# An encoder block on one core: the values' low halves on VectorE, the last four value blocks tile by tile, and a bank for the keys' products

## What is computed

```python
A = jnp.where(strict, jnp.einsum('nbhid,nbhjd->nbhij', k_beta, k) * dec, 0.0)
attn = jnp.einsum('nbhid,nbhjd->nbhij', q, k) * dec
```

```python
act = jax.nn.gelu(jnp.einsum('ld,lkd->lk', xb, u_tab[e]), approximate=False)
y = jnp.einsum('lk,lkd->ld', act * g, v_tab[e])      # summed over heads
h = layer_norm(DEEPNORM_ALPHA * h + y, ln2_g, ln2_b)
return h[:, N_META:]
```

## Time and profile before

| | us |
|---|---|
| median of 3 runs (lowest to highest) | 2587.49 (2587.34 to 2589.34) |
| the profiled execution, and its span | 2584.99, 2583.2 |
| TensorE busy (matmuls) | 2412.5, 93% |
| VectorE, GpSimd, ScalarE busy | 1821.2, 1245.4, 1002.5 |
| value stage | from 2031 to 2583 of the span |
| delta stage, heads in the loop | 78 a head |

### The profile page before, as it was taken

How to read it: one execution, slowest core, us unless ns; L and a number is a source line. 1 busy time by engine, 2 the same in 40 slices (tenths; PEclk the granted TensorE clock), 3 DMA queues, 4 the chain that set the end, 5 groups by cost and what they waited for, 6 DMA issues and landing times. The chain is left out here.

```text
span 2583.2 us, 44561 instructions
## 1 busy us (share of the span) xinstructions
PE 2412.5 (93%) x14900; PEld 1436.5 (56%) x14993; DVE 1821.2 (71%) x3471; ACT 1002.5 (39%) x1759; POOL 1245.4 (48%) x740
## 2 busy tenths in 40 slices
PE   7999999979999999988999999989898899999997
PEld 5444444458888878874465555555565444444442
DVE  7534422047777777752432898889999699999999
ACT  3332332223333333323313333338888333333332
POOL 4321331321222121214513676666677588888885
PEclk9999999999999999999999999999999999999998
DMA  5321322221110001004321587778999799999996
GB/s 205 98 66 32 98 65 71 66 72 34 33 32 32 8 24 32 8 1 131 114 99 54 192 287 255 240 231 296 383 362 369 260 331 335 333 334 333 335 331 235
DMA packets 174309, 440.32 MB, mean 170 GB/s; under 512 B 17408, under 2 KB 83584, under 8 KB 174096
## 3 DMA queue, kind: packets, MB, share of 16 engines
q1 hardware_dynamic: 132752, 288.20, 32.5%
q0 software_dynamic: 36864, 134.23, 15.6%
q10 hardware_dynamic: 4608, 16.78, 1.6%
HBM read 395.11 MB, written 44.04 MB: 170 GB/s over the span
## 5 line engine op out<-in xcount | busy, mean ns | idle before, releaser
L2040 POOL TENSOR_TENSOR hid_u_lo<-hid_u,hid_u_hi 128x1024 bf16<-128x1024 f32 x128 | 295.4, 2308 | 195.6 <-ACT hid_u_hi L2024 183.0
L150 PE MATMUL bank<-hT_hi,hid_u_hi 128*128 128x384 bf16 x1024 | 335.3, 327 | 17.2 <-POOL hid_u_lo L2040 5.8
L214 POOL TENSOR_TENSOR w_shared_lo<-w_raw,w_shared_hi 128x1024 bf16<-128x1024 f32 x72 | 157.9, 2210 | 393.5 <-ACT w_shared_hi L209 393.5
L150 PE MATMUL bank<-hT_hi,hid_u_lo 128*128 128x384 bf16 x1024 | 335.0, 327 | 0.0
L150 PE MATMUL bank<-hT_lo,hid_u_hi 128*128 128x384 bf16 x1024 | 335.0, 327 | 0.0
L2786 DVE TENSOR_TENSOR ex_gated<-ex_gated,ex_grid 128x128 f32<-128x128 f32 x128 | 277.3, 2166 | 0.0
L150 PE MATMUL bank<-hT_hi,w_shared_hi 128*128 128x264 bf16 (+2 forms) x699 | 200.8, 295 | 7.6 <-ACT dn_conv_in L1419 4.5
L150 PE MATMUL bank<-hT_lo,w_shared_hi 128*128 128x264 bf16 (+2 forms) x699 | 200.7, 295 | 1.4 <-ACT ex_grid L2216 1.2
L150 PE MATMUL bank<-hT_hi,w_shared_lo 128*128 128x264 bf16 (+2 forms) x699 | 200.7, 295 | 0.3
L2739 ACT ACTIVATE ex_gated_hi<-ex_gated 128x384 bf16<-128x384 f32 x128 | 66.9, 522 | 340.8 <-DVE ex_gated L2786 340.8
L2754 POOL TENSOR_TENSOR w_shared_lo<-ex_v,w_shared_hi 128x1024 bf16<-128x1024 f32 x64 | 152.5, 2383 | 47.3 <-ACT w_shared_hi L2736 47.3
(11 more groups left out here) (507 smaller groups left out, 6084.1 us busy)
## 6 DMA issues: line engine op xcount, KB each, us to landing
hid_u<-in_peer_u SPq DMA_DIRECT2D x128, 512.0 KB
ex_v<-in_peer_v SPq DMA_DIRECT2D x128, 512.0 KB, 5.5
w_raw<-in_w_ret SPq DMA_DIRECT2D x60, 512.0 KB, 4.3
expert_hidden<-hid_gelu SPq DMA_DIRECT2D x128, 192.0 KB
ex_gated<-expert_hidden SPq DMA_DIRECT2D x128, 192.0 KB
w_raw<-in_w_dn SPq DMA_DIRECT2D x32, 512.0 KB, 3.5
expert_weights<-ex_grid ACTq DMA_DIRECT2D x32, 512.0 KB
ex_weights<-expert_weights SPq DMA_DIRECT2D x64, 256.0 KB
```

What stands on the lines that cost most here:

```text
L150: last = nc.tensor.matmul(out, left[l], right[r], start=start and i == 0, stop=stop and i == len(PASSES) - 1)
L214: self.nc.gpsimd.tensor_tensor(self.pairs[slot][1][:, m % 4, :, :], self.raw[:, m % self.RING, :, :], self.pairs[slot][0][:, m % 4, :, :], ...
L2040: self.nc.gpsimd.tensor_tensor(self.us[1][:, m % 2, :, :], self.u32[:, m % RING, :, :], self.us[0][:, m % 2, :, :], ALU.subtract).then_inc ...
```

## The change

In the value stage:

- VectorE makes the values' low half, in each step between the row addition and the gated low half. GpSimd's stream keeps the 128 gathers alone.
- A row is added two steps behind (`BEHIND`), so that two are left after the last step.
- TensorE takes the first 124 blocks as before. The last four (`LAST`) it takes unit by unit: all four blocks for tile 0's first half, then for its second, and so on, and it signals `summed` after each unit.
- A tile's normalisation follows its own moments.

In the delta stage `kk` moves from bank 1 to bank 5, `qk` comes after the meta tokens' product, and ScalarE copies `tk` ahead of `tv`.

```diff
         early = Banks(core, [("q", 2), ("pm0", 3), ("k", 3), ("pm1", 5), ("v", 5), ("pm2", 2), ("bf", 2),
-                             ("bb", 3), ("bm", 5), ("nq", 2), ("nk", 3), ("nm", 5), ("ss", 6), ("z", 6)], DH)
-        order = [("tv", 1), ("tk", 4), ("tm", 7), ("kk", 1), ("qk", 4), ("kkm", 7)]
+                             ("bb", 3), ("bm", 5), ("nq", 2), ("nk", 3), ("nm", 5), ("ss", 6), ("z", 6), ("kk", 5)], DH)
+        order = [("tv", 1), ("tk", 4), ("tm", 7), ("qk", 4), ("kkm", 7)]
...
-                        for name, dst in (("tv", v_tok), ("tk", k_tok)):
+                        for name, dst in (("tk", k_tok), ("tv", v_tok)):
...
+    BEHIND = 2
+    LAST = 4
...
+                def products(u, slot, ends):
+
+                    half, t = UNITS[u]
+                    for i, (l, r) in enumerate(PASSES):
+                        last = nc.tensor.matmul(core.banks[u][:, :], gs[l][:, slot, t * P:(t + 1) * P],
+                                                vs[r][slot][:, half * 512:(half + 1) * 512],
+                                                start=False, stop=ends and i == 2)
+                    return last
+
                 def step(n, m):
-                    last_one = isinstance(n, int) and n == BLOCKS - 1
-                    slot = m % SLOTS
+                    if isinstance(n, int) and n >= BLOCKS - LAST:
+                        return
                     for name in ("gated_hi", "gated_lo", "v_hi", "v_lo"):
                         pe.wait_ge(s[name], n + 1)
...
+                for u in range(len(UNITS)):
+                    for n in range(BLOCKS - LAST, BLOCKS):
+                        if u == 0:
+                            for name in ("gated_hi", "gated_lo", "v_hi", "v_lo"):
+                                pe.wait_ge(s[name], n + 1)
+                        last = products(u, n % SLOTS, n == BLOCKS - 1)
+                    last.then_inc(s["summed"], 1)
...
-                def low_half(n):
-                    pool.wait_ge(s["v_hi"], n + 1)
-                    nc.gpsimd.tensor_tensor(vs[1][n % SLOTS], v32[:, n % RING, :], vs[0][n % SLOTS],
-                                            ALU.subtract).then_inc(s["v_lo"], 1)
-
-                low_half(0)
...
-                    if n:
-                        low_half(n)
...
-                    if m:
-                        add_row(n - 1, m - 1 if m > 1 else 0)
+                    if m >= BEHIND:
+                        add_row(n - BEHIND, m - BEHIND)
+                    dve.wait_ge(s["v_hi"], n + 1)
+                    nc.vector.tensor_tensor(vs[1][m % SLOTS], v32[:, m % RING, :], vs[0][m % SLOTS],
+                                            ALU.subtract).then_inc(s["v_lo"], 1)
...
-                add_row(BLOCKS - 1, BLOCKS - 1)
+                for n in range(BLOCKS - BEHIND, BLOCKS):
+                    add_row(n, n)
...
                 for turn, tile in enumerate(ORDER):
                     moments(turn, tile)
-                    if turn == 1:
+                    if turn == 0:
                         dve.wait_ge(s["gb_in"], 32 + SPENT)
-                    if turn:
-                        normalise(turn - 1, ORDER[turn - 1])
-                normalise(NT - 1, ORDER[NT - 1])
+                    normalise(turn, tile)
```

More of the change, by code:

```diff
@@ L1225, in unit @@
                     early.wait_read(pe, "nq", h)
-                    for name, i in (("kk", 1), ("qk", 0)):
-                        bk.wait_free(pe, name, h)
-                        for t in range(NT):
-                            last = nc.tensor.matmul(out(name)[:, t * P:(t + 1) * P], qk[:, 1, tok_cols(t)],
-                                                    qk[:, i, tok_cols(t)], start=True, stop=True)
-                        bk.fills(name, last)
+                    early.wait_free(pe, "kk", h)
+                    for t in range(NT):
+                        last = nc.tensor.matmul(out("kk")[:, t * P:(t + 1) * P], qk[:, 1, tok_cols(t)],
+                                                qk[:, 1, tok_cols(t)], start=True, stop=True)
+                    early.fills("kk", last)
                     bk.wait_free(pe, "kkm", h)
@@ L1234, in unit @@
                                                      qk[:, 1, 0:META], start=True, stop=True))
+                    bk.wait_free(pe, "qk", h)
+                    for t in range(NT):
+                        last = nc.tensor.matmul(out("qk")[:, t * P:(t + 1) * P], qk[:, 1, tok_cols(t)],
+                                                qk[:, 0, tok_cols(t)], start=True, stop=True)
+                    bk.fills("qk", last)
                 def following(part, hn, at_start):
@@ L1538, in turn @@
                             .then_inc(s["qd_ready"], 1)
-                    bk.wait_read(pool, "kk", h)
+                    early.wait_read(pool, "kk", h)
                     bk.wait_read(pool, "kkm", h)
@@ L1581, in matrices @@
                     dve.wait_ge(s["dec_ready"], 2 * h + 2)
-                    bk.wait_full(dve, "kk", h)
+                    early.wait_full(dve, "kk", h)
                     for i, d in enumerate(DIRS):
@@ L1587, in matrices @@
                                 in1=dec[:, i, c, :], op0=ALU.mult, op1=ALU.mult)
-                    bk.reads("kk", ins)
+                    early.reads("kk", ins)
                     bk.wait_full(dve, "kkm", h)
@@ L2711, in _ @@
             def _(pe):
+                def products(u, slot, ends):
[5 more added lines that the diff above has]
+                    return last
                 def step(n, m):
-                    last_one = isinstance(n, int) and n == BLOCKS - 1
-                    slot = m % SLOTS
+                    if isinstance(n, int) and n >= BLOCKS - LAST:
+                        return
                     for name in ("gated_hi", "gated_lo", "v_hi", "v_lo"):
                         pe.wait_ge(s[name], n + 1)
-                    for u, (half, t) in enumerate(UNITS):
-                        for i, (l, r) in enumerate(PASSES):
-                            last = nc.tensor.matmul(core.banks[u][:, :], gs[l][:, slot, t * P:(t + 1) * P],
-                                                    vs[r][slot][:, half * 512:(half + 1) * 512],
-                                                    start=False, stop=last_one and i == 2)
-                        if last_one:
-                            last.then_inc(s["summed"], 1)
-                    if not last_one:
-                        last.then_inc(s["used"], 1)
-                run(pe, step)
+                    for u in range(len(UNITS)):
+                        last = products(u, m % SLOTS, False)
+                    last.then_inc(s["used"], 1)
+                run(pe, step)
+                for u in range(len(UNITS)):
+                    for n in range(BLOCKS - LAST, BLOCKS):
[4 more added lines that the diff above has]
+                    last.then_inc(s["summed"], 1)
             @block.scalar
```

## The result

The changed kernel takes 2547.01 us (median of 4 runs, 2546.72 to 2549.06) where the kernel before takes 2587.41 beside it: a ratio of 0.9848, 95% interval 0.9833 to 0.9862. The forecast was 2551.0 in a range of 2541 to 2566. The profiled execution took 2547.08 us with a span of 2545.3.

What follows compares the result with a forecast made beforehand. VectorE, locked with GpSimd, was taken to bound the value stage; afterwards the transfers. A span of 2549.7 less 3 for the keys' products is 2546.7; plus 1.8 and 2.5 gives 2551.0 us, range 2541 to 2566.

Steps and rivals of the forecast that it cites:

- The lock on line 2786: Value stage: VectorE's product stands still until GpSimd's low half ends, 1.93 us of each 4.13 us step.
- the low half: Value stage: the subtraction of 128 x 1024, moved to VectorE, costs 1.14 us a block, bounds 1.07 and 2.40.
- VectorE's step without waits: Value stage: VectorE's step becomes 3.34 us, under TensorE's 3.88 us a block.
- Transfers at 353 GB/s: Value stage: full DMA engines become the bound, 3.90 us a step; chance 0.52 for 344 to 359 GB/s.
- T: Value stage: the moment VectorE has finished block 127, put at 2524.3 us, set by the transfers.
- rival (a): Value stage: transfers keep up and TensorE is the bound, span 2540.0, median 2541.3 us; chance 0.26.
- the first gather's earlier start: Value stage's start: first gather issued some 1.8 us before today's 2034.29, so DMA engines fill from about 2032.5.
- The end: Last four blocks: reordering costs 3.1 us if VectorE comes just in time; it pays only with a lead.
- Keys' products: Delta stage: products moved to bank 5 no longer wait for ScalarE's copy; 3 us gained, between 1.9 and 9.
- Rival (c): Value stage: VectorE and GpSimd's gathers exclude each other, step 4.43 us, median 2625 us; chance 0.05 in full.

Runs made afterwards that it cites:

- block 0 by passes: Changed kernel with four row buffers instead of eight, plus TensorE taking block 0 pass by pass: 2541.16 us, against 2540.57 without the passes.

## Why the prediction was right, and where it was not

**The lock on line 2786: right.** Its successor, line 2795, takes 0.28 us (mean 285 ns), and the low half costs VectorE 1.14 us until the next operation starts (2484.68 to 2485.82), as estimated. VectorE's step without waits is 3.34 us (2045.16 to 2048.50), to the hundredth. The added reader on GpSimd brings the lock back, so the cause is shown.

**Transfers at 353 GB/s: the step that failed.** The term divided a rate by a share, took the result, 347, for nearly the capacity and moved only a third of the way to a full stretch's 372. Measured: 389. So VectorE was through with block 127 at 2509.13 + 0.55 = 2509.7 and not at T = 2524.3 (2521.3 with the earlier stage), and TensorE, not the transfers, set the end, which was rival (a), to which the forecast gave 0.26. That the forecast's span (2546.7) is so near the measured one (2545.3) is luck, two errors that nearly cancel: VectorE's end 11.6 us too late, and the way from there to the end 10.2 us too short (25.4 against 35.6).

**Rival (a)'s own sum.** It said 2541.3 and missed by 5.7. Its terms against the trace, with the 3 us of the earlier stage taken off: first matmul 2030.6, came 2032.28 (+1.7, nearly all of it the start of the stage, which came 1.4 us earlier and not 3); first to last matmul 498.8 with the last one's own 0.2, came 505.4 (+6.6: 3.6 the hole, 2.4 the lower clock, at which 22 matmuls ran and not the ten of the sum, 0.6 a spacing of 0.2158 and not 0.2156); from there to the end 7.6, came 7.6. That is 8.3 more of span. The other way went the last step: 4.3 from span to median, of which only 1.7 was there, since the 2.5 us by which the kernel before's profiled run lay under its median were that run's chance.

**The hole.** The forecast named the first gather's earlier start as a gain, since the engines would fill sooner. It did not ask what eight gathers of 0.52 MB, issued one after the other, stand in front of. Until now each sat behind a low half of 2.40 us, so they could not leave together. Fewer gathers ahead take the hole away: shown by four traces in which TensorE waits nowhere but before its first matmul; the fifth, block 0 by passes, keeps the 1.61 us.

**The end.** "Costs 3.1 us if VectorE comes just in time; pays only with a lead": shown in direction by the kernels with and without it: 7.1 us of gain behind TensorE, and 1.5 us of cost (1.9 by the sum without the second row addition), the latter from one pair of traces. In the changed kernel the last matmul's distance to the end fell from 18.49 to 7.80.

**Keys' products: 3 us taken, 1.9 to 9 as bounds; 0.5 to 1 came.** TensorE's 18.1 us of waits did not go, they moved: the keys' own product waits for nothing now, but the meta tokens' product right behind it (line 1232) waits 16.8 us in 16 places for ScalarE's copy of the keys. VectorE's wait before line 1585 (now 1589) fell from 3.8 us in 8 places to 1.8 in 1, and still the state updates gain only 0.5 to 1 us. The step that failed is the lower bound: eight times 0.24 from the earlier trace rows supposed that a wait taken away before one operation is not given back before the next. VectorE's other waits in a head are for TensorE as well; which of them takes it back I did not follow.

**Rival (c), a lock between VectorE and the gathers:** VectorE is not held, its operations keep their durations; the gathers are stretched, from a mean of 0.95 to 1.53 us. In the changed kernel's trace the 48 gathers that start while VectorE is idle take 0.93 to 0.95 us each, the 77 that start during the values' low half (line 2799) 1.9 on average; before, 124 started during the row addition, whose sum lies in PSUM, and took 0.95. So what stretches them is the low half's presence; that it is the same lock is not shown. The row that the forecast held against (c), a gather of 1.09 us, was already a stretched one: it is one of two that started during line 2790. GpSimd has 2 us to spare a block, so it costs nothing.

## What to carry to other kernels

The DMA engines' share is no measure of what is left: take the rate from a stretch in which no engine is the bound, or make one by leaving work out, and look whether the loads themselves wait for a free buffer there. When a wait or an operation is removed, ask what had been spaced out by it: here eight transfers that used to leave one by one left together, ahead of those that were needed first. An edit of the end is worth what the engine that ends last makes of it, so it has to be judged together with the edit that decides which one that is.

## What the hardware showed that I had not expected

- One core alone reads 389 GB/s in this mix (0.5 MB and smaller loads, and gathers of rows), over hundreds of microseconds, with a share of 1.05.
- Beside a GpSimd subtraction of 128 x 1024 that touches none of VectorE's data, a VectorE product of 0.42 us takes 2.65; a memset of the same size, 0.97 us, holds none of 128.
- Behind a gap of 3.44 us TensorE's granted clock fell to the lower level for some 3 us (2062.47 to 2065.46); in another run of the same kernel, behind gaps of 3.1 us together, it did not.
- An indirect gather issued from GpSimd takes 0.94 us beside an idle VectorE and 1.9 on average when it starts during VectorE's subtraction of 128 x 1024; VectorE's own durations do not change.
- With identical code ahead of it, a stage two milliseconds into the kernel starts anywhere within 9 us (2027.21 to 2036.16) from one profiled execution to the next. A single pair of traces does not size an effect of 1 or 2 us there; lengths within a stage do (509.5 and 509.2 for the same kernel).
